# Modulation weights in the ring of weight units of a two-layer trunk kernel

## The chip, the cores and the metric

The kernel runs on one core of a Trainium2 chip. TensorE is PE, and its weight loads are listed apart as PEld; VectorE is DVE, ScalarE is ACT, SyncE is SP, which here does nothing but issue DMAs and wait for their slots. The metric is the device time of one execution in microseconds (us). TensorE's granted clock is given as a share of its full speed: 1.00 is 2.4 GHz, 0.50 is 1.2 GHz, and a value in between is a stretch with both.

## The reference

Two layers act on a prompt tile and a sample tile of 128 rows each, with 2048 channels. All weights are read once, in float32.

```
for l in range(2):
    sh1, sc1, g1, sh2, sc2, g2 = split(silu(cond) @ w_mod[l] + b_mod[l], 6)   # 2048 x 12288, two conditions
    h = rmsnorm(x) * (1 + sc1) + sh1
    q, k, v of A, B, C, and f = split(h @ w_in[l])                            # 2048 x 4352
    outs = attention A (8 heads), B (4 double heads), C (8 heads), Fourier mix of f
    merged = sum_b sigmoid(h @ w_gate[l][b] + b_gate) * (outs[b] @ w_branch[l][b])
    x = x + g1 * (merged @ w_out[l])
    h2 = rmsnorm(x) * (1 + sc2) + sh2
    x = x + g2 * mixture_of_16_experts(h2)                                    # top group, then 2 experts
```

The modulation is a product of two rows (the condition of the prompt and that of the sample) with a matrix of 96 MB for each layer. Its results are wanted late: sh1 and sc1 ahead of the layer's first norm, g1 in the rows of the merge (`gate_rows(32)`), sh2 and sc2 in the second norm, g2 in `gate_rows(80)` after it.

## The kernel before

**Weight units.** A weight matrix comes in units of 512 rows by 512 columns (128 partitions x 4 blocks x 512, 1 MB), four to a chunk of 512 output columns. SP's `load` puts each in one of 4 slots of `raw_w`. ACT rounds it to a high part (L557, two halves), DVE forms the low part (L872, two halves), both into one of 2 split slots, and PE runs 24 matmuls per unit, for each block and tile high x high, low x high and high x low (L1392 to L1394). A slot of `raw_w` comes free once DVE has made the low part (`low_ready`).

**Modulation units.** The matrix of the modulation is 24 chunks of 4 units per layer, 48 chunks and 192 units of 1 MB in all. They are not split: PE multiplies them as they land, four matmuls to a unit (L1412, in `mod_units`), each on its own 32 columns of the array, with the two conditions as weights. A chunk ends with a copy of its sums (`mod_copy`, DVE L879), a turn of four small matmuls on PE (`mod_turn`, L1420) and an add into `mod` (`mod_store`, DVE L885). They have a ring of their own, `mod_w` with 4 slots, in the memory of the split slots; so they are never in flight beside weight units, and `load_mods` waits until the split slots are used up.

**Stages.** Per layer: norm, w_in (8 chunks of 4 units and a last one of half the width), mixers (Fourier, then 12 groups of A, B and C, each a chain of scores, softmax, turn of the weights, values), gates (for each of 4 column chunks and each of 4 branches: 4 units of w_gate and one of w_branch), merge and `gate_rows`, w_out (4 chunks), routing (norm, router, `gate_rows`, sort), experts. Every engine runs its own program in this order. `mod_stage` and `MOD_ORDER` lay down where the chunks go: 8 at the start; in the mixers 14 per layer (2 beside Fourier, 12 beside the groups, one chunk to a group: two units ahead of the turn of the weights, two behind it); in layer 0 also 2 beside the merge, 2 beside its rows and 8 beside norm, rows and sort of the routing; in layer 1 two beside the norm of the routing. `mod_step` on PE and DVE places them there.

Of the kernel before, what the change touches and what calls it, by code (L numbers as in the profile page):

```python
# [37 lines left out]
F32 = mybir.dt.float32  # L38
# [14 lines left out]
MOD_SLOTS = 4  # L53
# [101 lines left out]
def trunk(nc, io, places):  # L155
# [12 lines left out]

    FIRST = 2 * D // COLS

    def mod_stage(l, stage):
        spans = {"fourier": [(l, FIRST, FIRST + 2)], "attention": [(l, FIRST + 2, MODS - 2)]}
        if l + 1 < DEPTH:
            spans |= {"merge": [(l, MODS - 2, MODS)], "mixer rows": [(l + 1, 0, 2)], "norm": [(l + 1, 2, FIRST - 4)],
                      "expert rows": [(l + 1, FIRST - 4, FIRST - 2)], "sort": [(l + 1, FIRST - 2, FIRST)]}
        else:
            spans |= {"norm": [(l, MODS - 2, MODS)]}
        return [(m, c) for m, a, b in spans.get(stage, []) for c in range(a, b)]

    STAGES = ("fourier", "attention", "merge", "mixer rows", "norm", "expert rows", "sort")  # L180
    MOD_ORDER = [(0, c) for c in range(FIRST)] + [m for l in range(DEPTH) for s in STAGES for m in mod_stage(l, s)]
# [9 lines left out]
    with ExitStack() as ctx:  # L191
# [14 lines left out]
        mod_w = place("mod_w", [P, MOD_SLOTS, KB, COLS], at=spot[0] - 4 * MOD_SLOTS * KB * COLS)  # L206
# [35 lines left out]
        mod = place("mod", [P, 2, MODS * 4, 2])  # L242
# [45 lines left out]
        turn_banks, mod_bank = banks[5:7], banks[7]  # L288
# [5 lines left out]
        high_ready, low_ready, unit_used = sem("high_ready"), sem("low_ready"), sem("unit_used")  # L294
        chunk_read, gate_ready = sem("chunk_read"), sem("gate_ready")
        mod_in = [sem(f"mod_in{i}") for i in range(MOD_SLOTS)]
        mod_used, mod_copied, mod_turned, mod_stored = sem("mod_used"), sem("mod_copied"), sem("mod_turned"), sem("mod_stored")
# [81 lines left out]
        def _(sp):  # L379
            at = Cursor()  # L380

            def load(src, width=COLS):
                slot = at.parity("unit", RAW_SLOTS)
                u = at.next("unit")
                need(sp, low_ready, (u - RAW_SLOTS + 1) * HALVES)
                at.next(f"in{slot}")
                sp.dma_start(raw_w[:, slot, :, 0:width], src).then_inc(raw_in[slot], 16)

            def load_mod(l, c):

                for j in range(UPC):
                    slot = at.parity("mod_unit", MOD_SLOTS)
                    need(sp, mod_used, at.next("mod_unit") - MOD_SLOTS + 1)
                    sp.dma_start(mod_w[:, slot, :, :], weight_tile(io["w_mod"], l, bass.ds(c * COLS, COLS), COLS, j)
                                 ).then_inc(mod_in[slot], 16)

            def load_mods(chunks):

                need(sp, unit_used, (at.done("unit") - UPC) * HALVES if chunks else 0)
                for l, c in chunks:  # L400
                    load_mod(l, c)

# [14 lines left out]

            def mod_start(c):
                load_mod(0, c)
            at.rounds(sp, FIRST, mod_start)  # L420
            sp.dma_start(proj[0:36, 0, 0:4 * P], io["pick"][0:36, :]).then_inc(pick_in, 16)
# [6 lines left out]
            for l in range(DEPTH):  # L428
# [29 lines left out]
                def mixers():  # L458
# [8 lines left out]
                    beside = mod_stage(l, "fourier") + mod_stage(l, "attention")  # L467
                    early = 2 + 6
                    load_mods(beside[:early])

# [3 lines left out]
                    load_mods(beside[early:])  # L474


                def gates(n):
                    for b in range(4):
                        for j in range(UPC):
                            load(weight_tile(io["w_gate"], l, bass.ds(n * COLS + b * D, COLS), COLS, j))  # L480
                        if b == 0:
                            r = at.next("bg")
                            if at.first:
                                mixers()
                                sp.wait_ge(bg_clear, l + 1)
# [8 lines left out]
                def merge():  # L494
# [4 lines left out]
                    load_mods(mod_stage(l, "merge") + mod_stage(l, "mixer rows"))  # L499

                def w_out(n):
                    for j in range(UPC):
                        load(weight_tile(io["w_out"], l, bass.ds(n * COLS, COLS), COLS, j))
# [4 lines left out]
                def routing():  # L508
                    sp.dma_start(numbers[:, :], io["numbers"]).then_inc(numbers_in, 16)
                    load_mods(mod_stage(l, "norm") + mod_stage(l, "expert rows") + mod_stage(l, "sort"))  # L510

                def experts(i):
                    for h in range(2):
                        for j in range(UPC):
                            slot = at.parity("unit", RAW_SLOTS)
                            u = at.next("unit")
                            need(sp, low_ready, (u - RAW_SLOTS + 1) * HALVES)
                            for half, name in enumerate(("w_exp_gate", "w_exp_up")):
                                at.next(f"in{slot}")
# [24 lines left out]
        def _(act):  # L544
            at = Cursor()

            def split_high(width=COLS, loads=1):

                slot, part = at.parity("unit", RAW_SLOTS), at.parity("unit", SPLIT_SLOTS)
# [9 lines left out]
            def mods_done():  # L559

                act.wait_ge(mod_used, mods_done.units)
            mods_done.units = UPC * FIRST

# [23 lines left out]

            for l in range(DEPTH):
# [1249 lines left out]
```

## Time and profile before

| | us |
|---|---|
| median of 3 runs | 3095.6 (3092.16 to 3099.6) |
| span of the profiled execution | 3096.7 |
| PE busy | 2766.8 (89% of the span) |
| DVE busy | 1577.1 (51%) |
| ACT busy | 1248.2 (40%) |
| 16 DMA engines busy with the main queue | 66.2% of the span |
| moved | 689.73 MB, mean 223 GB/s |

The profiled execution's span, from the first to the last instruction, is its own time as the trace has it; it lies inside the spread of the three runs, 1.1 us above their median. The shares are means over stages of different kinds, so the rows below are cut by stage. A row of the windows view gives start and end of a stretch, its length, the busy time and instruction count of PE, PEld, DVE, ACT and POOL, then the granted clock, the DMA engines' busy share and the rate. In a timeline, the bracket at a row's end is the time that the engine stood idle ahead of it, and what ended that.

### The profile page before, as it was taken

The numbers are of one execution on the slowest core, as the hardware profiler recorded it, in microseconds if no ns is written. First come the engines' busy times: TensorE is split into PE (matmuls) and PEld (weight loads), VectorE is DVE, ScalarE is ACT, GpSimd is POOL, SyncE is SP. The second block draws the span as 40 slices with busy tenths as digits, with TensorE's granted clock in tenths as the row PEclk, the third lists the DMA queues.
The fourth block names the chain that finished last, engine by engine and source line by source line (L and its number), as shares of the span: only waits on it lengthen the run. The fifth ranks groups of instructions, "written<-read, shape, count | busy, mean of one in ns | idle before, by whom it ended". The sixth has DMA issues, their size and how long they took to land.

```text
span 3096.7 us, 35968 instructions
## 1 busy us (share of the span) xinstructions
PE 2766.8 (89%) x13006; PEld 2069.3 (67%) x13007; DVE 1577.1 (51%) x2058; ACT 1248.2 (40%) x1645; POOL 0.2 (0%) x4
## 2 busy tenths in 40 slices
PE   5799778999998987999978987799999988799997
PEld 1488345888884754787766863478888866677775
DVE  0444333455543545768655433244555454576875
ACT  0244233434442323546544423334444332355654
POOL 0000000000000000000000000000000000000000
PEclk8799889999999978999988999899999988799998
DMA  9755987555558565869764579855555536186974
GB/s 363 246 195 174 339 304 253 182 192 189 187 178 287 177 226 187 269 212 321 257 219 151 193 241 327 298 187 187 190 187 183 187 122 206 46 270 220 323 256 176
DMA packets 428973, 689.73 MB, mean 223 GB/s; under 512 B 26796, under 2 KB 163788, under 8 KB 428208
## 3 DMA queue, kind: packets, MB, share of 16 engines
q1 hardware_dynamic: 428848, 687.96, 66.2%
q8 instruction: 91, 1.49, 0.2%
q14 instruction: 34, 0.28, 0.0%
HBM read 683.45 MB, written 4.46 MB: 222 GB/s over the span
## 4 chain that ended last, share of the span: by engine, by line
PE 75%; DMA 10%; DVE 7%; issue 3%; ACT 3%; DVEq 2%; SPq 1%; ACTq 0%
PE bank L1392 16%; PE bank L1393 15%; PE bank L1394 15%; DMA mod_w<-in_w_mod 10%; PE bank L1412 4%; PE bank L1737 3%; PE bank L1739 3%; PE bank L1738 3%; DVE low_w L872 3%; PE bank L1430 2%; PE bank L1779 2%; PE bank L1780 2%; PE bank L1781 2%; PE bank L1468 1%; ACT high_w L557 1%
## 5 line engine op out<-in xcount | busy, mean ns | idle before, releaser
L872 DVE TENSOR_TENSOR low_w<-raw_w,high_w 128x1024 fp32r<-128x1024 f32 (+1 forms) x912 | 1083.4, 1213 | 795.9 <-ACT high_w L557 790.3
L557 ACT ACTIVATE high_w<-raw_w 128x1024 fp32r<-128x1024 f32 (+1 forms) x912 | 941.8, 1052 | 869.6 <-PE bank L1394 670.9
L1392 PE MATMUL bank<-high_w,in_high 128*128 128x512 f32 (+1 forms) x1856 | 724.6, 390 | 20.4 <-DVE low_w L872 20.4
L1394 PE MATMUL bank<-high_w,in_low 128*128 128x512 f32 (+1 forms) x1856 | 720.6, 388 | 0.0
L1393 PE MATMUL bank<-low_w,in_high 128*128 128x512 f32 (+1 forms) x1856 | 720.6, 388 | 0.0
L1392 PEld LDWEIGHTS bank<-high_w,in_high 128*128 128x128 f32 x1856 | 351.9, 190 | 104.2 <-issue 33.9
L1394 PEld LDWEIGHTS bank<-high_w,in_low 128*128 128x128 f32 x1856 | 351.4, 189 | 71.2
L1393 PEld LDWEIGHTS bank<-low_w,in_high 128*128 128x128 f32 x1856 | 352.0, 190 | 70.0
L1412 PE MATMUL bank<-mod_w,cond 128*32 128x512 f32 x1536 | 257.4, 768 | 94.8 <-DMA mod_w<-in_w_mod 86.2
L1737 PE MATMUL bank<-high_w,in_high 128*128 128x512 f32 x640 | 258.9, 404 | 29.2 <-DVE low_w L872 29.0
L1739 PE MATMUL bank<-high_w,in_low 128*128 128x512 f32 x640 | 251.8, 393 | 0.0
L1738 PE MATMUL bank<-low_w,in_high 128*128 128x512 f32 x640 | 251.8, 393 | 0.0
L1412 PEld LDWEIGHTS bank<-mod_w,cond 128*32 128x32 f32 x1536 | 38.1, 122 | 216.5 <-DMA mod_w<-in_w_mod 134.6
L1737 PEld LDWEIGHTS bank<-high_w,in_high 128*128 128x128 f32 x640 | 121.3, 190 | 69.9 <-DVE low_w L872 41.7
L879 DVE COPY mod_sums<-bank 128x512 f32<-128x512 f32 x48 | 33.2, 691 | 251.9 <-PE bank L1412 251.9
L1739 PEld LDWEIGHTS bank<-high_w,in_low 128*128 128x128 f32 x640 | 121.3, 190 | 26.6
L1738 PEld LDWEIGHTS bank<-low_w,in_high 128*128 128x128 f32 x640 | 121.4, 190 | 23.5
L1779 PE MATMUL bank<-high_w,hid_high 128*128 128x512 f32 x320 | 127.1, 397 | 6.6 <-DVE low_w L872 6.6
L1780 PE MATMUL bank<-low_w,hid_high 128*128 128x512 f32 x320 | 126.3, 395 | 0.0
L1781 PE MATMUL bank<-high_w,hid_low 128*128 128x512 f32 x320 | 126.0, 394 | 0.0
L724 ACT ACTIVATE sig<-bank 128x256 f32<-128x256 f32 (+1 forms) x128 | 55.5, 486 | 172.5 <-PE bank L1394 168.4
L1392 PE MATMUL bank<-high_w,br_high 128*128 128x512 f32 x256 | 99.6, 389 | 0.0
(208 smaller groups left out, 2113.0 us busy)
## 6 DMA issues: line engine op xcount, KB each, us to landing
mod_w<-in_w_mod SPq DMA_DIRECT2D x192, 1024.0 KB, 8.7
raw_w<-in_w_gate SPq DMA_DIRECT2D x128, 1024.0 KB, 5.1
raw_w<-in_w_in SPq DMA_DIRECT2D x64, 1024.0 KB, 5.3
raw_w<-in_w_exp_gate SPq DMA_DIRECT2D x128, 512.0 KB, 4.5
raw_w<-in_w_exp_up SPq DMA_DIRECT2D x128, 512.0 KB, 5.5
raw_w<-in_w_exp_down SPq DMA_DIRECT2D x64, 1024.0 KB, 6.3
raw_w<-in_w_branch SPq DMA_DIRECT2D x32, 1024.0 KB, 5.1
raw_w<-in_w_out SPq DMA_DIRECT2D x32, 1024.0 KB, 5.1
```

What stands on the lines that cost most here:

```text
L557: act.activation(high_w[:, part, ks, 0:width], raw_w[:, slot, ks, 0:width], ACT.Copy).then_inc(high_ready, 1)
L872: dve.tensor_tensor(low_w[:, part, ks, 0:width], raw_w[:, slot, ks, 0:width], high_w[:, part, ks, 0:width].bitcast(F32), ALU.subtract).the ...
L1392: pe.matmul(out, highs[:, kk, t, :], high_w[:, part, k, 0:width], start=start, stop=False)
L1393: pe.matmul(out, highs[:, kk, t, :], low_w[:, part, k, 0:width], start=False, stop=False)
L1394: done = pe.matmul(out, lows[:, kk, t, :], high_w[:, part, k, 0:width], start=False, stop=stop)
L1412: done = pe.matmul(mod_bank[32 * k:32 * k + 32, :], cond[:, j * KB + k, :], mod_w[:, slot, k, :], start=j == 0, stop=j == UPC - 1)
L1737: pe.matmul(out, in_high[:, kk, t, :], high_w[:, part, k, :], start=kk == 0, stop=False)
L1738: pe.matmul(out, in_high[:, kk, t, :], low_w[:, part, k, :], start=False, stop=False)
L1739: done = pe.matmul(out, in_low[:, kk, t, :], high_w[:, part, k, :], start=False, stop=kk == NK - 1)
L1779: pe.matmul(out, hid_high[:, kk, t, :], high_w[:, part, k, :], start=False, stop=False)
L1780: pe.matmul(out, hid_high[:, kk, t, :], low_w[:, part, k, :], start=False, stop=False)
L1781: done = pe.matmul(out, hid_low[:, kk, t, :], high_w[:, part, k, :], start=False, stop=False)
```

## The change

The modulation units lose their own ring and go through the 4 slots of `raw_w`, in line with the weight units, in places written out in three tables. In every chunk of w_in in both layers, and of w_out in layer 0, the order is m0 w0 m1 m2 w1 m3 w2 w3 (m: a unit of modulation, w: of the weight). In the gates it is m0 w0 m1 w1 m2 w2 m3 w3 and then the unit of w_branch, for the first three of the four branches in layer 0 and the first two in layer 1. With the 8 chunks at the start, that makes 8 + 8 + 12 + 4 in or ahead of layer 0 and 8 + 8 in layer 1. Mixers, merge, rows and routing have none. A slot is now freed by a semaphore of its own (`raw_done`): for a weight unit by DVE's low part, for a modulation unit by PE's last matmul on it. `mod_turn` writes to another bank. The matrix is laid out anew ahead of the launch, so that a unit is one block of memory, 8 KB per partition instead of four rows of 2 KB. The load of `pick` stands ahead of the first modulation units, and `mixers` on SP (stores of the new caches, loads of `cache_bc`) stands after the first four units of the gates, not after the first four of w_gate.

```diff
-        mod_w = place("mod_w", [P, MOD_SLOTS, KB, COLS], at=spot[0] - 4 * MOD_SLOTS * KB * COLS)
+    MOD_BEFORE = [(0,), (1, 2), (3,), ()]
+    GATE_MODS = [3] + [2] * (DEPTH - 1)
+    OUT_MODS = [1] + [0] * (DEPTH - 1)
...
             def load(src, width=COLS):
-                slot = at.parity("unit", RAW_SLOTS)
-                u = at.next("unit")
-                need(sp, low_ready, (u - RAW_SLOTS + 1) * HALVES)
-                at.next(f"in{slot}")
+                slot = at.parity("ring", RAW_SLOTS)
+                at.next("ring")
+                need(sp, raw_done[slot], at.next(f"use{slot}") * HALVES)
                 sp.dma_start(raw_w[:, slot, :, 0:width], src).then_inc(raw_in[slot], 16)
...
+            def load_mod(j):
+                m = at.done("mod_chunk")
+                if j == UPC - 1:
+                    at.next("mod_chunk")
+                load(io["w_mod"][bass.ds(m, 1), j].rearrange("a p (k n) -> p (a k) n", k=KB))
...
                         for j in range(UPC):
+                            for m in MOD_BEFORE[j]:
+                                load_mod(m)
                             load(weight_tile(io["w_in"], l, bass.ds((i * 2 + h) * COLS, COLS), COLS, j))
...
                         for j in range(UPC):
+                            if b < GATE_MODS[l]:
+                                load_mod(j)
                             load(weight_tile(io["w_gate"], l, bass.ds(n * COLS + b * D, COLS), COLS, j))
+                            if b == 0 and at.first and j == 1:
+                                mixers()
...
-            def mod_copy():
+            def mod_copy(slot, later):
                 m = at.next("mod_copy")
-                dve.wait_ge(mod_used, m * UPC + UPC)
+                dve.wait_ge(raw_done[slot], (at.done(f"use{slot}") - later) * HALVES)
                 need(dve, mod_turned, m)
                 dve.tensor_copy(mod_sums[:, :], mod_bank[:, :]).then_inc(mod_copied, 1)
...
                 for j in range(blocks // KB):
+                    for m in mods[j] if mods else ():
+                        mod_unit(m)
                     part, u = at.parity("unit", SPLIT_SLOTS), at.next("unit")
+                    slot, use = ring_slot()
+                    at.next(f"in{slot}")
                     for k in range(KB):
                         if k % HALF == 0:
-                            pe.wait_ge(low_ready, u * HALVES + k // HALF + 1)
+                            pe.wait_ge(raw_done[slot], use * HALVES + k // HALF + 1)
...
+                    if j == 2 and mods is MOD_BEFORE:
+                        mod_turn()
...
+            def mod_unit(j):
+                slot, use = ring_slot()
+                if j == 0:
+                    need(pe, mod_copied, at.next("mod_chunk"))
+                pe.wait_ge(raw_in[slot], at.next(f"in{slot}") * 16 + 16)
+                for k in range(KB):
+                    done = pe.matmul(mod_bank[32 * k:32 * k + 32, :], cond[:, j * KB + k, :], raw_w[:, slot, k, :],
+                                     start=j == 0, stop=j == UPC - 1)
+                done.then_inc(raw_done[slot], HALVES)
...
                 for G, (j, b, t, g) in enumerate(GROUPS):
                     if G + 1 < NG:
                         scores(G + 1)
-                    mod_step(2)
                     turn_weights(G)
-                    mod_units(UPC - 2)
                     values(G)
-                    mod_step(0)
...
+    arrays["w_mod"] = np.ascontiguousarray(blocks.transpose(0, 4, 1, 3, 2, 5)).reshape(-1, d // (KB * P), P, KB * COLS)
```

PE's program in the first chunk of w_in, layer 0, after the change, from the chunk's start to the turn (a unit that landed in `raw_w` is multiplied by `cond` for the modulation, and by `in_high` and `in_low` after its split; L1424 is the turn):

```order
L1414 MATMUL bank<-raw_w,cond 32x512 x4
L1391 MATMUL bank<-high_w,in_high 128x512
L1392 MATMUL bank<-low_w,in_high 128x512
L1393 MATMUL bank<-high_w,in_low 128x512
...
L1414 MATMUL bank<-raw_w,cond 32x512 x8
...
L1424 MATMUL bank<-const,mod_sums 128x2 x4
```

m0, the pair m1 and m2, and the turn are new there, with 24 matmuls of a weight unit wherever rows are left out (m3 stands ahead of the third weight unit like m0 ahead of the first); before, PE's rows in w_in are the same triples, with line numbers one higher, without a break. PE's program at the head of the mixers of layer 0, before (L1501, L1508 and L1509 are the Fourier mix, L1430 turns, L1551 the scores, L1590 the values, L1412 and L1420 the modulation):

```order
L1501 MATMUL bank<-const,proj 128x256 x4
L1412 MATMUL bank<-mod_w,cond 32x512 x16
L1508 MATMUL bank<-e_buf,const 128x512
L1509 MATMUL bank<-e_buf,const 128x512
L1501 MATMUL bank<-const,proj 128x256 x4
L1420 MATMUL bank<-const,mod_sums 128x2 x4
L1412 MATMUL bank<-mod_w,cond 32x512 x16
L1508 MATMUL bank<-e_buf,const 128x512
L1509 MATMUL bank<-e_buf,const 128x512
L1420 MATMUL bank<-const,mod_sums 128x2 x4
L1430 MATMUL bank<-const,proj 128x128 x5
```

And after, from the same place to the values of the first group:

```order
L1497 MATMUL bank<-const,proj 128x256 x4
L1503 MATMUL bank<-e_buf,const 128x512
L1504 MATMUL bank<-e_buf,const 128x512
L1497 MATMUL bank<-const,proj 128x256 x4
L1503 MATMUL bank<-e_buf,const 128x512
L1504 MATMUL bank<-e_buf,const 128x512
L1428 MATMUL bank<-const,proj 128x128 x5
L1428 MATMUL bank<-const,cache_a 128x128
L1546 MATMUL bank<-qk_t 128x128 x16
L1428 MATMUL bank<-const,e_buf 128x128 x8
L1585 MATMUL bank<-p_t,cache_a 64x128
```

The modulation is gone from between the steps of the chain. SP's program from the end of w_in to the first gates of layer 0, before:

```order
L387 DMA raw_w<-in_w_gate 128x4x512 [waits low_ready] x4
L466 DMA out_new_attn_k<-proj 128x128 [waits chunk_read]
...
L394 DMA mod_w<-in_w_mod 128x4x512 [waits mod_used,unit_used]
L394 DMA mod_w<-in_w_mod 128x4x512 [waits mod_used] x31
L472 DMA cache_bc<-in_cache_na_k 128x512 [waits pv_done]
L473 DMA cache_bc<-in_cache_na_v 128x512
L394 DMA mod_w<-in_w_mod 128x4x512 [waits mod_used,unit_used]
L394 DMA mod_w<-in_w_mod 128x4x512 [waits mod_used] x23
L488 DMA bg_raw<-in_b_gate 4x512 [waits bg_clear]
```

And after:

```order
L379 DMA raw_w<-in_w_mod 128x2048 [waits raw_done0]
L379 DMA raw_w<-in_w_gate 128x4x512 [waits raw_done1]
L379 DMA raw_w<-in_w_mod 128x2048 [waits raw_done2]
L379 DMA raw_w<-in_w_gate 128x4x512 [waits raw_done3]
L454 DMA out_new_attn_k<-proj 128x128 [waits chunk_read]
...
L456 DMA cache_bc<-in_cache_na_k 128x512 [waits pv_done]
L457 DMA cache_bc<-in_cache_na_v 128x512
L379 DMA raw_w<-in_w_mod 128x2048 [waits raw_done0]
L379 DMA raw_w<-in_w_gate 128x4x512 [waits raw_done1]
L379 DMA raw_w<-in_w_mod 128x2048 [waits raw_done2]
L379 DMA raw_w<-in_w_gate 128x4x512 [waits raw_done3]
```

The 56 modulation loads of the mixers are gone from the queue, and two units of modulation and two of w_gate lie in the ring while the mixers run, where there were four of w_gate.

## Rows read from the trace of the kernel before

**Rows 1.** The page: the chain that ended last, shares of the span by line.
```profile
PE bank L1392 16%; PE bank L1393 15%; PE bank L1394 15%; DMA mod_w<-in_w_mod 10%; PE bank L1412 4%; PE bank L1737 3%; PE bank L1739 3%; PE bank L1738 3%; DVE low_w L872 3%; PE bank L1430 2%; PE bank L1779 2%; PE bank L1780 2%; PE bank L1781 2%; PE bank L1468 1%; ACT high_w L557 1%
```

**Rows 2.** Busy by stretch: PE, PEld, DVE, ACT, POOL; clock, DMA share, GB/s.
```profile
0.00:102.90 102.90, 64.69 (x324) 19.29 (x325) 8.61 (x24) 7.60 (x9) 0.20 (x4) 0.78 1.00 364
102.90:126.40 23.50, 8.38 (x33) 6.04 (x33) 19.86 (x47) 7.41 (x11) 0.00 (x0) 0.52 0.63 184
...
315.20:506.10 190.90, 142.59 (x983) 72.31 (x984) 60.82 (x154) 56.30 (x178) 0.00 (x0) 0.85 0.88 317
506.10:960.30 454.20, 451.47 (x1952) 364.89 (x1952) 228.30 (x207) 182.10 (x195) 0.00 (x0) 1.00 0.58 186
960.30:1012.90 52.60, 38.92 (x208) 13.43 (x208) 16.70 (x51) 12.67 (x20) 0.00 (x0) 0.86 0.86 313
...
1105.70:1225.90 120.20, 91.26 (x527) 51.98 (x527) 53.76 (x164) 31.04 (x49) 0.00 (x0) 0.74 0.60 207
...
1831.20:2026.60 195.40, 145.80 (x984) 73.25 (x984) 60.68 (x154) 56.56 (x178) 0.00 (x0) 0.83 0.86 310
...
2481.90:2506.20 24.30, 16.39 (x48) 8.31 (x48) 13.69 (x43) 11.73 (x19) 0.00 (x0) 0.72 0.00 0
...
2597.90:2696.90 99.00, 72.74 (x366) 50.70 (x367) 51.12 (x157) 30.26 (x48) 0.00 (x0) 0.67 0.23 82
```

**Rows 3.** The chain in the mixers of layer 0, shares by line.
```profile
by line: DMA mod_w<-in_w_mod 54.4%; PE bank L1412 14.4%; PE bank L1551 5.2%; PE bank L1430 2.6%; PE bank L1553 2.4%; PE bank L1420 2.0%; ACT e_buf L676 1.9%; SPq L394 1.8%; PE bank L1587 1.5%; issue 1.5%; SPq L466 1.3%; ACT qk_t L661 1.3%; 
```

**Rows 4.** Timeline, mixers of layer 0: start, duration, instruction, idle before.
```profile
334.42 1.86 PE L1508 MATMUL bank<-e_buf,const 128*128 128x512 f32 x2
...
344.36 1.13 PE L1508 MATMUL bank<-e_buf,const 128*128 128x512 f32 x2
...
355.30 0.16 DVE L1045 TENSOR_TENSOR small<-small 128x4 f32<-128x4 f32 x1 [2.09 <-ACT e_buf L676]
...
363.36 1.05 PE L1420 MATMUL bank<-const,mod_sums 128*128 128x2 f32 x8
...
364.53 0.16 DVE L1045 TENSOR_TENSOR small<-small 128x4 f32<-128x4 f32 x1
```

**Rows 5.** As rows 2: the same 24 score matmuls of branch C, twice.
```profile
441.65:445.88 4.23, 4.23 (x24) 3.26 (x25) 0.00 (x0) 0.00 (x0) 0.00 (x0) 1.00 0.53 196
455.57:463.06 7.49, 7.49 (x25) 5.69 (x24) 2.12 (x4) 1.26 (x1) 0.00 (x0) 0.50 0.54 198
```

**Rows 6.** PE's timeline in the first stage: two modulation units.
```profile
17.76 1.93 PE L1412 MATMUL bank<-mod_w,cond 128*32 128x512 f32 x8 [0.69 <-DMA mod_w<-in_w_mod]
20.47 1.94 PE L1412 MATMUL bank<-mod_w,cond 128*32 128x512 f32 x8 [0.78 <-DMA mod_w<-in_w_mod]
```

**Rows 7.** DMA issues: count, KB each, median us to landing.
```profile
raw_w<-in_w_in SPq DMA_DIRECT2D x64, 1024.0 KB, 5.3
...
x<-in_x_prompt SPq DMA_DIRECT2D x1, 1024.0 KB, 4.9
x<-in_x_sample SPq DMA_DIRECT2D x1, 1024.0 KB, 6.9
```

**Rows 8.** PE's timeline in the sort, layer 0: two periods, with one unit each.
```profile
1202.09 0.72 PE L1684 MATMUL bank<-sort,turned_high 128*128 128x256 f32 x4
...
1205.06 0.72 PE L1684 MATMUL bank<-sort,turned_high 128*128 128x256 f32 x4
```

**Rows 9.** PE's timeline in the sort, layer 1: two periods without units.
```profile
2682.20 0.72 PE L1684 MATMUL bank<-sort,turned_high 128*128 128x256 f32 x4
...
2684.03 0.72 PE L1684 MATMUL bank<-sort,turned_high 128*128 128x256 f32 x4
```

**Rows 10.** PE's timeline: three units back to back.
```profile
339.91 2.78 PE L1412 MATMUL bank<-mod_w,cond 128*32 128x512 f32 x24 [0.26 <-DVE mod L885]
```

**Rows 11.** The page's groups: splitting a weight unit, count, busy, mean ns.
```profile
L872 DVE TENSOR_TENSOR low_w<-raw_w,high_w 128x1024 fp32r<-128x1024 f32 (+1 forms) x912 | 1083.4, 1213 | 795.9 <-ACT high_w L557 790.3
L557 ACT ACTIVATE high_w<-raw_w 128x1024 fp32r<-128x1024 f32 (+1 forms) x912 | 941.8, 1052 | 869.6 <-PE bank L1394 670.9
```

More of the change, by code:

```diff
@@ L241, in trunk @@
         pick = place("pick", [36, 4, P], F32R)
-        mod = place("mod", [P, 2, MODS * 4, 2])
+        mod = place("mod", [P, DEPTH, MODS * 4, 2])
         gains = place("gains", [P, 2 * DEPTH, NK])
@@ L547, in split_high @@
             def split_high(width=COLS, loads=1):
-                slot, part = at.parity("unit", RAW_SLOTS), at.parity("unit", SPLIT_SLOTS)
+                slot, part = at.parity("ring", RAW_SLOTS), at.parity("unit", SPLIT_SLOTS)
+                at.next("ring")
                 u = at.next("unit")
@@ L557, in split_high, with pass_mods @@
                     act.activation(high_w[:, part, ks, 0:width], raw_w[:, slot, ks, 0:width], ACT.Copy).then_inc(high_ready, 1)
-            def mods_done():
-                act.wait_ge(mod_used, mods_done.units)
-            mods_done.units = UPC * FIRST
+            def pass_mods(units):
+                for _ in range(units):
+                    slot = at.parity("ring", RAW_SLOTS)
+                    at.next("ring")
+                    at.next(f"in{slot}")
             def root_mean_square():
@@ L758, in _ @@
                 gate_rows()
-                mods_done.units += UPC * len(mod_stage(l, "merge") + mod_stage(l, "mixer rows"))
-                mods_done()
                 def w_out(n):
                     for j in range(UPC):
+                        if OUT_MODS[l]:
+                            pass_mods(len(MOD_BEFORE[j]))
                         split_high()
@@ L799, in _ @@
                     act.activation(in_high[:, 2 * q:2 * q + 2, :, :].rearrange("p k t n -> p (k t n)"), banks[2][:, :], ACT.Copy).then_inc(sort_stored[0], 1)
-                mods_done.units += UPC * len(mod_stage(l, "norm") + mod_stage(l, "expert rows") + mod_stage(l, "sort"))
-                mods_done()
                 def hid_copy(e):
@@ L865, in split_low @@
             def split_low(width=COLS):
-                slot, part = at.parity("unit", RAW_SLOTS), at.parity("unit", SPLIT_SLOTS)
+                slot, part = at.parity("ring", RAW_SLOTS), at.parity("unit", SPLIT_SLOTS)
+                at.next("ring")
+                at.next(f"use{slot}")
                 u = at.next("unit")
@@ L902, in root_mean_square, with norm @@
                 dve.wait_ge(root_ready, n + 1)
-            def norm(l, which, mod_units=0):
+            def norm(l, which):
                 shift, scale, gain = 48 * which, 48 * which + 16, 2 * l + which
@@ L963, in w_in_pair @@
                 def w_in_pair(i):
-                    for j in range(2 * UPC):
-                        split_low()
-                    at.next("chunk")
-                    at.next("chunk")
+                    for h in range(2):
+                        for j in range(UPC):
+                            pass_mods(len(MOD_BEFORE[j]))
+                            if 3 in MOD_BEFORE[j]:
+                                last = pass_mods.slot
+                            split_low()
+                            if j == 2:
+                                mod_copy(last, 0)
+                        mod_store()
+                        at.next("chunk")
                 at.rounds(dve, IN_CHUNKS // 2, w_in_pair)
@@ L1118, in gates @@
                             at.next(f"merge{l}")
+                        for j in range(2):
+                            pass_mods(mods)
+                            split_low()
+                        if mods:
+                            mod_copy(pass_mods.slot, 0)
                         split_low()
-                        split_low()
-                        split_low()
+                        if mods:
+                            mod_store()
                 at.at[f"merge{l}"] = -1
@@ L1480, in mod_start @@
             def mod_start(c):
-                mod_units(UPC)
+                for j in range(UPC):
+                    mod_unit(j)
                 mod_turn()
```

208 lines of the change are left out of this document (87 added, 121 removed).

## The prediction

> **What bounds the kernel now.** First the page's chain: over 60% of the span are matmuls on weight units, and one tenth is waiting for modulation loads, with 4% more for their matmuls [rows 1]. So there are two kinds of stage, and a mean over the span hides them. The windows, cut at the stages, part them [rows 2]. In the gates of layer 0 PE is busy 451.5 of 454.2 us at clock 1.00 and the DMA engines 0.58 of the time: PE sets the pace, and whatever is put on PE there comes on top. In the mixers (190.9 us in layer 0, 195.4 in layer 1) the DMA engines are busy 0.88 and 0.86 of the time while the clock is below 0.86. The chain inside the mixers of layer 0 says what holds them: 54.4% waiting for modulation loads, 14.4% their matmuls, 2.0% the turns [rows 3]. Mixers, the merge and routing of layer 0 have room on PE and lack bandwidth; w_in, gates and w_out have bandwidth and no room on PE. The change moves 160 of the 192 modulation units (40 chunks) from the former to the latter. The question is which is dearer.
>
> **What the move gives back.** *Mixers.* How long are they bare? I walked the timeline of layer 0 along the chain scores, softmax, turn, values, and left out every stretch in which PE had nothing but modulation to wait for. The first 40.1 us, from 315.2 [rows 2] to the softmax weights of the first group at 355.30, hold two such stretches: the inputs of the two Fourier matmuls at 334.42 and 344.36 had been ready for 15.9 and 4.2 us [rows 4]. That leaves 20.0. The first group, 355.30 to 364.53, takes 9.2, and its modulation work lies under ACT and DVE [rows 4]; the 12 groups so walked are 105.7 in all, from 4.4 to 18.4 each. Sum: 126 us, with PE at 2.4 GHz almost throughout.
>
> It need not stay there. PE would be busy some 41 of these 126 us. The stretches that already run without modulation have this sort of load, and a low clock: 0.52 in the norm of layer 0 (PE busy 8.4 of 23.5), 0.72 in the merge and rows of layer 1 (16.4 of 24.3) [rows 2]. The same 24 score matmuls took 4.23 us at clock 1.00 and 7.49 at 0.50 [rows 5], a factor of 1.77; all of the 41 us at half speed would add 31, and make 157. I take two thirds of that, 147, since the two rows named are on average between the levels, nearer to the lower. Gain 190.9 - 147 = 44 and 195.4 - 147 = 48, together 92 (72 to 134).
>
> What speaks against the change stands in the Trainium skill, "TensorE: Matmul & The Clock Gate", Part 1: the throttled state is the default, and activity releases it. The rows agree (0.52 with PE idle most of the stretch); by that rule alone the mixers would be at 157 each, and the time 20 us longer than my sum.
>
> *Merge and rows of layer 0.* Those of layer 1 are the same work without modulation: 52.6 against 24.3 [rows 2], gain 28.
>
> *Routing.* Layer 0 has 32 units beside it, layer 1 has 8: 120.2 and 99.0 [rows 2]. 24 units with their turns thus cost 21.2, or 0.88 each; by that the bare routing is 92. By the sort, a period with a unit takes 2.97 (1202.09 to 1205.06) [rows 8] and one without 1.83 (2682.20 to 2684.03) [rows 9], so 1.14 each, and 8 of them with two turns at the low clock 0.67 are some 14: bare 85. If the clock stayed up it would be about 79. I take 85: gain 35 + 14 = 49 (35 to 61, by the three values).
>
> *Start.* The 32 units there follow each other at 2.71 us (17.76, 20.47), each ended by its load [rows 6]. Units of 8 KB rows were not in the trace, but x is loaded so: two loads one behind the other landed 4.9 and 6.9 us after their issue [rows 7], and one DMA kind is a little faster than the other. Between nothing and 0.25 us per unit (8 us), I take 6.
>
> Gain in all: 92 + 28 + 49 + 6 = 175 (135 to 231).
>
> **What it costs.** *A unit on PE.* Three back to back take 2.78, so 0.93 each [rows 10]; in the sort, between matmuls of the full array as it will stand now, 1.14 [rows 8, 9]. The new places are of the second kind, so m0 and m3 of a w_in chunk and all four in a gates chunk are 1.14, and the pair m1 m2 is 2.0. *A turn* is 1.05 in its row [rows 4], some of it under its neighbours: 1.0. A w_in or w_out chunk: 1.14 + 2.0 + 1.14 + 1.0 = 5.28; there are 8 + 8 + 4 = 20, so 106. A gates chunk: 4 x 1.14 + 1.0 = 5.56; there are 12 + 8 = 20, so 111. Sum 217; with every unit and turn at 0.93 it is 186.
>
> *The ring.* Where PE needs a weight unit, its load, its high and its low half must be done: 5.3 from issue to landing [rows 7], then 1.05 on ACT and 1.21 on DVE for the first half [rows 11]. In a w_in chunk the slot of w1 was m0's, free only when PE has finished m0. Counted from the chunk's start, PE ends m0 at 1.14; w1 is split at 1.14 + 0.1 + 5.3 + 1.05 + 1.21 = 8.8. PE comes to it after m0, w0, m1 and m2: 1.14 + 5.5 + 2.0 = 8.6. (A weight unit takes about 5.5: the gates' 454.2 over 80 units is 5.68, and holds the bias matmuls too [rows 2].) Likewise w2 in the slot of m1, 15.3 against 15.2. So loads are just late, by some 0.2 twice per chunk: 20 x 0.4 = 8. If loads took as long as the second of x, 6.9, each would be 1.6 later: 20 x 3.6 = 72. The rate that is asked, 8 MB per chunk of some 27 us (310 GB/s), is below what the start moves, 364 [rows 2]. In the gates w_j sits in the slot of w_(j-2), free as soon as DVE has split that, so there is no such wait. I take 8 (0 to 72).
>
> The page "DMA: Bandwidth & Descriptors" of the Trainium skill, Anatomy of one DMA, would give 2.0 us plus the bytes over 436 GB/s, an estimate of 4.4 us per load, where the rows show 5.3 to 6.9. By it the ring would never wait, and the time would be 8 lower.
>
> *Other edits, at nothing.* The copy of the sums and the add to `mod` wait on DVE, ahead of later splits; in w_in the copy stands behind the low part of w2, about the time that PE ends m3, and the low part of w3 has 24 matmuls of w2 to hide under. PE's turn stands behind that same unit, so the copy is done. In the gates the copy is behind w3's low part, and PE has w3 to do before the turn. If a copy came late, PE would wait what remains of it, under 1 us in each of 40 chunks. The first two units of w_gate were in the ring during the mixers before and still are; the other two now load once the mixers are over, while PE works on m0, w0 and m1, w1, more than 13 us against a load of 5.3. The moved load of `pick` and the stores of the caches stand ahead of work that PE reaches tens of us later.
>
> Sum: 217 + 8 - 175 = +50. On the trace's own span of 3096.7 that is 3147; the span lies 1 above the median of the runs shown, so I say **3145**.
>
> **The rivals.** *The clock stays up in the mixers.* Then they take 126 each and the routing 79: gains 65 + 69 + 28 + 61 + 6 = 229 against 225, so 3093, not slower; with units at 0.93 too it is 3062. It decides where the mixers come under 128 us each. For it: the clock was 0.85 with modulation between, and the bare chain is denser than the present one. Against it: 0.52 and 0.72 in the stretches without modulation [rows 2]. *The clock is low throughout.* Mixers 157, routing 92: gains 141, time 3181. For it the norm's 0.52, against it the merge's 0.72. *The ring starves.* Loads of 6.9 us where two ask at once make the 72 above in place of 8, so 3209, or with half of it 3177. For it: the DMA engines would be asked for over 80% of what the start moves. Against it: at the start they deliver 364 GB/s without a gap. *Units on PE are cheap.* If a unit between fp32r matmuls costs 0.93, the sum is 31 lower, 3116; for it rows 10, against it rows 8 and 9, whose place is more alike.
>
> **How the numbers follow.** My forecast with the cheap units as its lower end, 3110 to 3170: 0.55. Clock up: 0.20, of which 0.14 under 3089. Clock low throughout: 0.12. Ring starving: 0.10. What is left, 0.03, is faster for several of the reasons at once. From the case of the clock the range takes in the half from 3070 up, from the low clock and the ring what lies up to 3190: 3070 to 3190. A measurement of this kernel tells a difference from about 0.2%, or 6 us. Faster by more: 0.14 + 0.03 = 0.17. Within it: 0.05, the upper part of the clock case. Slower: 0.78.
>
> **What would show it.** Mixers of 140 to 155 us each, without a wait for a modulation load, and a granted clock of 0.55 to 0.75 there; merge and rows of layer 0 at 24; routing near 85 in both layers. The gates of layer 0 longer by 12 x 5.56 = 67, those of layer 1 by 44, w_in of either layer by 42 to 46, w_out of layer 0 by 21, with clock 1.00. In w_in PE should wait for low parts of w1 and w2 for tenths of a us. A clock near 0.9 in the mixers would turn the sign of the forecast; waits of a us or more at w1 and w2 would say that the ring starves; a period of a modulation unit under 1 us between weight units would say that I overpriced it.

## The result

The changed kernel takes 3201.6 us (median of 4 runs, 3195.9 to 3207.0), the kernel before 3097.6 in the runs beside it: a ratio of 1.0334, 95% interval 1.0307 to 1.0361. It is slower, as forecast, but by 104 us and not by 50, and outside the range, which ended at 3190.

The windows of the changed kernel, cut at the same events as [rows 2]: the start with the first norm, w_in, mixers, gates, merge and routing of layer 0, then mixers, gates and routing of layer 1.

```profile
0.00:120.10 120.10, 70.95 (x356) 23.45 (x357) 27.06 (x67) 13.36 (x18) 0.20 (x4) 0.74 0.83 337
120.10:360.60 240.50, 233.50 (x1184) 168.34 (x1184) 86.54 (x88) 76.67 (x90) 0.00 (x0) 0.99 0.82 294
360.60:498.10 137.50, 78.95 (x423) 60.54 (x423) 47.36 (x123) 53.78 (x175) 0.00 (x0) 0.65 0.04 13
498.10:1053.10 555.00, 526.89 (x2432) 385.79 (x2432) 237.14 (x233) 181.27 (x197) 0.00 (x0) 0.97 0.68 242
1053.10:1074.60 21.50, 16.46 (x50) 8.43 (x50) 12.45 (x41) 8.85 (x15) 0.00 (x0) 0.68 0.00 0
...
1192.10:1275.90 83.80, 58.85 (x287) 49.31 (x287) 49.61 (x152) 30.04 (x49) 0.00 (x0) 0.65 0.00 1
...
1930.40:2068.80 138.40, 81.39 (x425) 62.75 (x425) 47.37 (x124) 53.81 (x175) 0.00 (x0) 0.63 0.04 13
2068.80:2604.20 535.40, 507.27 (x2273) 382.75 (x2273) 234.63 (x225) 182.36 (x197) 0.00 (x0) 0.96 0.64 220
...
2719.60:2803.80 84.20, 59.13 (x287) 50.02 (x287) 49.71 (x152) 30.15 (x49) 0.00 (x0) 0.66 0.00 1
```

Read the lengths first, against [rows 2]. The mixers went from 190.9 to 137.5 and from 195.4 to 138.4, with the DMA engines busy 0.04 and the clock at 0.65 and 0.63. Merge and rows went from 52.6 to 21.5, routing from 120.2 to 83.8 and from 99.0 to 84.2. The gates of layer 0 went from 454.2 to 555.0, 101 more, where the sum had 67; and PE, busy 451.5 of 454.2 before, is now idle for 28 us of them, with a clock of 0.97. Those idle 28 us are no modulation unit's price: they are a wait. The view of PE's waits in that stretch (us in total, times, longest):

```profile
PE bank L1391 <- DVE low_w L858: 25.3, 4, 7.3
PE bank L1414 <- DVE br_low L998: 0.9, 1, 0.9
```

Four times, once per column chunk, PE waits for the low part of w2: 4.4 us in the first chunk, 6.8 to 7.3 in the other three. Layer 1 has the same (25.4 us in 4), and its gates went from 455.3 to 535.4, 80 more, where the sum had 44. The chain through the same stretch names, at 4.5% (25 us), something that the prediction never priced, the load of the gate bias:

```profile
by line: PE bank L1391 27.6%; PE bank L1392 25.4%; PE bank L1393 25.4%; PE bank L1414 8.1%; DMA bg_raw<-in_b_gate 4.5%; PE bank L1609 1.9%; PE bank L1424 1.7%; issue 1.0%; DVE low_w L858 0.9%; SPq L379 0.8%; DVE prod L1082 0.5%; DVEq L1084 
```

The timeline around the second of the four waits, SP's issues first, then the other engines:

```profile
636.22 0.34 SPq L379 DMA_DIRECT2D raw_w<-in_w_mod  x1
...
642.88 0.35 SPq L379 DMA_DIRECT2D raw_w<-in_w_mod  x1
643.41 1.47 SPq L379 DMA_DIRECT2D raw_w<-in_w_gate  x1
644.98 0.72 SPq L473 DMA_DIRECT2D bg_raw<-in_b_gate  x2
```

```profile
648.29 1.07 PE L1414 MATMUL bank<-raw_w,cond 128*32 128x512 f32 x8
...
651.12 0.63 ACT L725 ACTIVATE bg_split<-bg_raw 36x512 fp32r<-36x512 f32 x1 [15.00 <-DMA bg_raw<-in_b_gate]
651.65 3.88 ACT L542 ACTIVATE high_w<-raw_w 128x1024 fp32r<-128x1024 f32 x4
651.78 0.68 DVE L1103 TENSOR_TENSOR bg_split<-bg_raw,bg_split 4x512 fp32r<-4x512 f32 x1 [14.41 <-ACT bg_split L725]
...
656.60 0.80 PE L1391 MATMUL bank<-high_w,in_high 128*128 128x512 f32 x1 [7.25 <-DVE low_w L858]
657.20 0.63 PE L1392 MATMUL bank<-low_w,in_high 128*128 128x512 f32 x1
...
661.89 0.39 PE L1391 MATMUL bank<-high_w,in_high 128*128 128x512 f32 x1
```

SP issues the bias of a column chunk behind the units of its first branch. Before, these were four units of w_gate, each slot free as soon as a unit was split. Now they are eight, and m3 waits for the slot of m1, which PE gives back at 642.7. So the bias goes out at 644.98 and ACT has it at 651.12. ACT takes it ahead of splitting w2, and had stood idle for 15.0 us; DVE too takes it, and a merge, ahead of the low part of w2. PE, done with m2 at 649.35, gets w2 at 656.60. After the wait it starts at the low clock (granted 0.50 from 656.6 to 661.4; 0.63 per matmul, 0.43 apart) and is back at 0.39 per matmul only at 661.9. In the kernel before the same load was out 9.4 us ahead of its use, and ACT came to it without idle time:

```profile
611.93 0.71 SPq L488 DMA_DIRECT2D bg_raw<-in_b_gate  x2
```

```profile
621.38 0.61 ACT L738 ACTIVATE bg_split<-bg_raw 36x512 fp32r<-36x512 f32 x1
```

### The profile page after: what moved, and what is told of

Same layout as the page of the kernel before. It is cut to its first block, busy times and chain, and to the rows that moved or that the text cites. A ratio compares the mean times of both kernels' runs of the same rounds, so it can differ in the third digit from the quotient of the medians.

```text
span 3204.6 us, 35850 instructions
## 1 busy us (share of the span) xinstructions
PE 2809.4 (88%) x13006; PEld 2100.7 (66%) x13007; DVE 1564.6 (49%) x2058; ACT 1233.9 (39%) x1645; POOL 0.2 (0%) x4
## 4 chain that ended last, share of the span: by engine, by line
PE 71%; DVE 9%; DMA 7%; ACT 5%; issue 3%; DVEq 3%; SPq 1%; ACTq 0%
PE bank L1391 14%; PE bank L1392 13%; PE bank L1393 13%; PE bank L1414 4%; DVE low_w L858 3%; PE bank L1732 3%; PE bank L1733 3%; PE bank L1734 3%; PE bank L1428 3%; DMA raw_w<-in_w_in 3%; DMA raw_w<-in_w_mod 2%; PE bank L1776 2%; PE bank L1777 2%; PE bank L1778 2%; ACT high_w L542 2%
## 5 line engine op out<-in xcount | busy, mean ns | idle before, releaser
L858 DVE TENSOR_TENSOR low_w<-raw_w,high_w 128x1024 fp32r<-128x1024 f32 (+1 forms) x912 | 1072.0, 1212 | 765.0 <-ACT high_w L542 758.9
L542 ACT ACTIVATE high_w<-raw_w 128x1024 fp32r<-128x1024 f32 (+1 forms) x912 | 928.5, 1049 | 1047.1 <-PE bank L1393 326.2
L1391 PE MATMUL bank<-high_w,in_high 128*128 128x512 f32 (+1 forms) x1856 | 747.2, 403 | 69.1 <-DVE low_w L858 68.6
L1414 PE MATMUL bank<-raw_w,cond 128*32 128x512 f32 x1536 | 220.9, 662 | 33.1 <-DMA raw_w<-in_w_mod 21.8
L1414 PEld LDWEIGHTS bank<-raw_w,cond 128*32 128x32 f32 x1536 | 34.0, 112 | 128.3 <-issue 70.7
```

Source lines behind the costliest of these rows:

```text
L542: act.activation(high_w[:, part, ks, 0:width], raw_w[:, slot, ks, 0:width], ACT.Copy).then_inc(high_ready, 1)
L858: dve.tensor_tensor(low_w[:, part, ks, 0:width], raw_w[:, slot, ks, 0:width], high_w[:, part, ks, 0:width].bitcast(F32), ALU.subtract).the ...
L1391: pe.matmul(out, highs[:, kk, t, :], high_w[:, part, k, 0:width], start=start, stop=False)
L1414: done = pe.matmul(mod_bank[32 * k:32 * k + 32, :], cond[:, j * KB + k, :], raw_w[:, slot, k, :], start=j == 0, stop=j == UPC - 1)
```

## Experiments

**The bias load early.** Theory A: the bias load is late, and that is the gates' excess. Theory B: w2 itself is late, because modulation units hold the slots. In the changed kernel only the place of one issue is moved:

```diff
-                        if b == 0:
+                            if b == 0 and j == 1:
                                 r = at.next("bg")
...
```

> The changed kernel, with the load of the gate bias (bg_raw) issued after w1 of the first branch of each column chunk, no longer after w3. Theory A, the bias is late: PE's stalls of about 7 us at the third weight unit of every column chunk (8 in all) fall under 1 us, the gates are some 35 us shorter in each layer (520 and 500), and the time is about 3202 - 70 = 3132, 1.1% above the kernel before. Theory B, the weight unit itself is late because modulation units hold its slot: the stalls stay, and the time is 3195 to 3205.

Measured 3135.5, ratio 1.0105 (1.0082 to 1.0128), 2.2% below the changed kernel's. Between the two ratios, and between the two profiled spans (3204.6 and 3133.4), lie 71 us; the medians, taken at different times, are 66 apart. The windows of mixers and gates of layer 0, then of layer 1:

```profile
356.90:494.80 137.90, 81.07 (x426) 62.29 (x426) 47.35 (x124) 53.80 (x175) 0.00 (x0) 0.61 0.04 13
494.80:1017.50 522.70, 519.95 (x2433) 381.05 (x2433) 237.85 (x233) 181.35 (x197) 0.00 (x0) 0.99 0.72 257
1894.10:2034.10 140.00, 83.64 (x423) 63.83 (x423) 47.36 (x123) 53.77 (x175) 0.00 (x0) 0.61 0.04 13
2034.10:2534.40 500.30, 497.50 (x2273) 375.84 (x2273) 235.46 (x225) 182.55 (x197) 0.00 (x0) 0.99 0.69 236
```

And all of PE's waits in the gates of layer 0:

```profile
PE bank L1428 <- DVE merged L1085: 2.8, 1, 2.8
PE bank L1414 <- DVE br_low L998: 0.9, 1, 0.9
```

The gates are 32 and 35 us shorter, 67 together, PE waits for no low part in them any more, and theory A stands, B falls. What is left over the gates before is 522.7 - 454.2 = 68.5 for 12 chunks, 5.7 each, against 5.56 in the sum.

**The bias load late, in the kernel before.** The same cause, without a modulation unit in the ring: the issue goes behind the first unit of the second branch.

```diff
-                        if b == 0:
+                            if b == 1 and j == 0:
                                 r = at.next("bg")
...
```

> The kernel before, with the load of the gate bias issued after the first unit of the second branch, two loads later; no modulation unit is in the ring. Theory A: PE stalls at the third weight unit of each of the 8 column chunks, by 2 to 6 us with what the clock takes to come back, so 16 to 50 us more: 3113 to 3147. Theory B: no change, 3091 to 3104.

Measured 3129.7, ratio 1.0083 (1.0060 to 1.0105). PE's waits in the gates of layer 0, first in the kernel before, then here:

```profile
PE bank L1392 <- DVE low_w L872: 2.0, 1, 2.0
...
PE bank L1393 <- DVE low_w L873: 10.5, 4, 2.9
```

The first of the four is the wait of 2.0 at the start of the gates, which was there before; the other three, 2.8 to 2.9 each, stand at the third weight unit of the second to fourth column chunk. The gates grew by 12 and 9 us, to 466.3 and 464.8. So a late bias alone makes the wait, as theory A has it, though a shorter one than in the changed kernel. Between the two profiled spans (3129.2 and 3096.7) lie 32.5 us; 11 of them are in the mixers of layer 0 (202.0 against 190.9, at a clock of 0.77 against 0.85), whose loads this edit leaves as they were; why is not settled.

**Filler on PE in the mixers.** Is the chain of the mixers slow because PE's clock is low there (theory C), or by ACT and DVE (theory D)? On top of the early bias load:

```diff
...
                         scores(G + 1)
+                    filler(8)
                     turn_weights(G)
+                    filler(8)
                     values(G)
```

> As the kernel with the early bias load, and in every group of the mixers 8 matmuls on data that lie there anyhow ahead of the turn of the weights and 8 ahead of the values, on a bank that nobody reads: no load and no wait is added, only work on PE where it waits. Theory C, the low clock holds the mixers: granted clock there from 0.65 to above 0.85, mixers from 137 to 120 to 128 us per layer, time 20 to 35 below the kernel with the early bias load. Theory D, the chain through ACT and DVE holds them and the clock matters little: mixers 137 to 150, time the same or up to 25 above.

Measured 3116.0, ratio 1.0044 (1.0030 to 1.0057), 19.5 below the kernel with the early bias load. The mixers:

```profile
356.90:488.90 132.00, 108.13 (x619) 83.57 (x619) 47.30 (x124) 53.69 (x175) 0.00 (x0) 0.90 0.04 14
1883.80:2013.70 129.90, 107.55 (x615) 82.54 (x615) 47.26 (x123) 53.66 (x175) 0.00 (x0) 0.89 0.04 14
```

The chain in the mixers of layer 0 (L1495 is the filler):

```profile
by line: PE bank L1495 29.0%; PE bank L1551 11.4%; PE bank L1428 8.3%; PE bank L1590 5.9%; ACT e_buf L665 5.1%; ACT qk_t L650 4.2%; PE bank L1553 4.2%; issue 3.2%; PE bank L1587 2.2%; DVE small L1018 2.1%; ACT L699 1.9%; ACT e_buf L695 1.7%
```

24 to 27 us more work on PE made the mixers 6 and 10 us shorter, with the clock at 0.90 and 0.89 for 0.61; the gates behind them are 2 shorter each (520.3 and 498.1). Theory C holds in kind, and D falls; the mixers end 2 to 4 us above what C gave. The filler itself holds 29.0% of the chain, 38 us, so the 16 us are what the higher clock gave less what the filler took, and the worth of the clock alone is not measured.

**The layout alone.** The kernel before with units of one block, 8 KB per partition:

```diff
-                    sp.dma_start(mod_w[:, slot, :, :], weight_tile(io["w_mod"], l, bass.ds(c * COLS, COLS), COLS, j)
+                    sp.dma_start(mod_w[:, slot, :, :], io["w_mod"][bass.ds(c + l * MODS, 1), j].rearrange("a p (k n) -> p (a k) n", k=KB)
...
```

> The kernel before, with nothing of the change but the layout of the modulation matrix (a unit is one block, 8 KB per partition). Theory E, the modulation loads are the bound at the start and in the mixers and come 0.2 us per unit sooner in 8 KB rows: start 6 shorter, mixers 10 to 14 each, time 3066 to 3075, ratio about 0.991. Theory F, only the start gains, since in the mixers the loads wait for slots as much as for bytes: 3088 to 3093.

Measured 3075.0, ratio 0.9897 (0.9878 to 0.9917). In the profiled execution the start with the norm is 120.7 (before 126.4), the mixers 186.0 and 191.3 (before 190.9 and 195.4). The start gained what was expected, the mixers 4 to 5 and not 10 to 14: by the stages between E and F, by the time at the upper end of E. The ratio is worth 32 us, the stages of this one execution 17; two executions of one kernel differ by as much (3066 to 3082 here), and the difference is not resolved further. This part of the change was worth having by itself.

**Thin modulation matmuls.** With the early bias load, what of the price is PE's own time?

```diff
+                n = 2 if thin else COLS
...
-                    done = pe.matmul(mod_bank[32 * k:32 * k + 32, :], cond[:, j * KB + k, :], raw_w[:, slot, k, :],
+                    done = pe.matmul(mod_bank[32 * k:32 * k + 32, 0:n], cond[:, j * KB + k, :], raw_w[:, slot, k, 0:n],
```

> The kernel with the early bias load, where each matmul of the 160 moved modulation units takes 2 columns in place of 512 (the rest of their product is left out); loads, slots, waits, copies and turns stay. Theory G, what is left of the cost is PE's own time: the gates of layer 0 fall from 523 to about 470, w_in from 238 to 200, and the time by about 160 x 0.85 = 136 to 3000. Theory H, the loads in the shared ring hold PE for a good part of it: w_in stays above 220 and the time above 3050.

Measured 3057.4, ratio 0.9868 (0.9844 to 0.9892). w_in and gates of layer 0, and PE's waits in that w_in:

```profile
120.20:354.20 234.00, 215.42 (x1184) 173.24 (x1184) 86.73 (x88) 77.01 (x90) 0.00 (x0) 0.95 0.83 302
490.80:975.40 484.60, 480.39 (x2433) 380.80 (x2433) 237.75 (x233) 181.27 (x197) 0.00 (x0) 0.99 0.78 278
```

```profile
PE bank L1391 <- DVE low_w L858: 16.6, 9, 2.2
```

Both theories hold, each in its place. In the gates 48 units took 38 us less (0.8 each), as G has it. In w_in the 32 units took only 4.6 less (234.0 against 238.6): PE comes earlier to w1, waits 2 us for it in nearly every chunk, and works through w1 partly at the low clock (0.95 over the stage). So in w_in, with its 8 units to a chunk, the ring (a slot freed, its load, its split) is hardly faster than PE, and the pace of about 28 us per chunk would stand nearly unchanged with cheaper units too. Whether the rate of the loads or the turn-round of one slot sets that pace, this run does not show.

**Another order in w_in.** To tell whether whose slot it is decides that wait:

```diff
-    MOD_BEFORE = [(0,), (1, 2), (3,), ()]
+    MOD_BEFORE = [(0,), (1,), (2, 3), ()]
```

> The kernel with the early bias load, with one table entry moved: w_in and w_out chunks go m0 w0 m1 w1 m2 m3 w2 w3, so that w1 stands in a slot that the split frees early, and only w2 still needs the slot of a modulation unit (m1). Theory I, as the prediction's ring term has it: the wait for w1 (0.84 us in a chunk) goes, the same work stays on PE, w_in 2 to 6 us shorter per layer, in all 5 to 15 below the 3135 of the kernel with the early bias load. Theory J, the ring is bound by the rate of the loads and not by whose slot is free: the wait stands at w2 in place of w1, and the time is the same within 3.

Measured 3133.4, ratio 1.0103 (1.0082 to 1.0125): no difference. PE's waits in w_in of layer 0 are 5.6 us in 9, as they were (5.5 in 9):

```profile
PE bank L1391 <- DVE low_w L858: 5.6, 9, 1.5
```

Now eight of the nine stand at w2; the longest, 1.5, is at w0 of the second chunk, where the changed kernel has one too. Theory I falls. Theory J is not shown by that, for w2 stands in the slot of m1 here, and the prediction's own count has it just late too.

**Sharing out.** If 137 us of mixers hold almost no load (DMA 0.04), and get shorter by work on PE, some modulation belongs there. The shared kernel puts 8 chunks per layer back, through the same ring, with the early bias load; 24 stay between weight units.

```diff
-    GATE_MODS = [3] + [2] * (DEPTH - 1)
+    GATE_MODS = [1] + [0] * (DEPTH - 1)
...
+    MIX_MODS = [[4, 4] + [2] * 12] * DEPTH
...
                         scores(G + 1)
+                    ended = mix_units(2 + G)
                     turn_weights(G)
                     values(G)
+                    if ended:
+                        mod_turn(mod_bank)
```

> The modulation shared out: with the early bias load, 8 chunks per layer go back into the mixers, through the same ring (4 units beside each Fourier half, 2 in each group), and only those 24 that find no place there stay between weight units (8 per w_in, 4 in the gates and 4 in w_out of layer 0). By theories A and C: 32 loads at 2.5 us fit under the mixers' 130, the clock there is above 0.8, so mixers of 125 to 135; gates of layer 0 at 477, of layer 1 as before at 455; the sum is 3103 - 61 - 61 (mixers) - 31 - 51 (merge, routing) - 6 (start) + 24 x 5.9 = 3035. If the loads hold the mixers after all: 150 each, 3070.

Measured 3048.5, ratio 0.9845 (0.9823 to 0.9867). The mixers of layer 0 and the gates:

```profile
358.80:500.80 142.00, 107.82 (x752) 62.96 (x752) 55.80 (x142) 55.37 (x176) 0.00 (x0) 0.86 0.65 242
500.80:974.70 473.90, 471.15 (x2104) 368.85 (x2105) 231.25 (x215) 182.23 (x195) 0.00 (x0) 1.00 0.64 215
```

32 units with their turns make the mixers only 4 longer than with none, while 8 chunks in w_in cost 50. PE waits for no modulation load in them. The length was misjudged by some 7: the clock came back (0.86), but units and turns hold 17.9% of the chain there, 25 us, and took it again.

**More of it in layer 0.** 12 chunks in the mixers of layer 0 and none in its gates: `MIX_MODS` with 40 units over the groups, `GATE_MODS = [0, 0]`.

> As the shared kernel, but 12 chunks in the mixers of layer 0 and none in the gates. 48 loads at 2.5 us are 120 of the mixers' 130: if they flow, mixers of 135 to 140 and the time 15 below the shared kernel; if the groups wait for them as before the change, mixers of 155 to 165 and the time 5 to 10 above it.

Measured 3052.4, ratio 0.9851 (0.9829 to 0.9873), not to be told from the shared kernel. The mixers and gates of layer 0:

```profile
357.00:520.40 163.40, 126.07 (x903) 71.91 (x903) 58.80 (x150) 55.97 (x178) 0.00 (x0) 0.86 0.80 312
520.40:975.70 455.30, 452.57 (x1952) 365.70 (x1952) 228.24 (x207) 182.73 (x195) 0.00 (x0) 0.99 0.58 187
```

Four chunks cost 21 us in the mixers and gave back 19 in the gates. The loads hold the mixers again, as the second case had it: waiting for modulation loads is 20.2% of the chain there.

**From w_in to the gates.** The shared kernel with the 16 chunks of w_in in the gates (`GATE_MODS = [3, 2]`, no modulation unit in w_in).

> The shared-out kernel, with the 16 chunks of w_in put between the units of the gates instead (three of four branches in layer 0, two in layer 1); w_in has none. In the gates a chunk cost 5.6 to 5.7, in w_in 6.2: by that 16 x 0.6 = 9 less, 3039 against 3048.5. If the units in w_in cost what they do on PE alone and the waits came from elsewhere, no difference.

Measured 3040.4, ratio 0.9801 (0.9779 to 0.9823): the best of all, 2% below the kernel before and 5% below the changed one, and 8 us below the shared kernel, where 9 were expected. w_in, mixers and gates of layer 0:

```profile
120.30:309.50 189.20, 188.43 (x865) 157.58 (x865) 82.40 (x72) 78.48 (x88) 0.00 (x0) 0.99 0.59 189
309.50:452.50 143.00, 108.69 (x751) 64.92 (x751) 55.47 (x142) 55.31 (x176) 0.00 (x0) 0.84 0.65 241
452.50:971.90 519.40, 516.18 (x2425) 379.29 (x2425) 236.28 (x231) 180.16 (x195) 0.00 (x0) 1.00 0.73 261
```

w_in is back at 189.2, 49.6 shorter than in the shared kernel, and the gates are 45.5 longer: 6.2 per chunk against 5.7.

## Why the prediction was right and wrong

**The step that failed** is "other edits, at nothing", and with it the gates' price, 67 and 44, which had PE's own time and no wait in it; measured were 101 and 80. The step followed the copy, the turn, `pick` and the cache stores through the queues, but not the bias load, which the diff does not touch. Four modulation units went in ahead of it in SP's queue, and what stands behind them in that queue was not listed. The wait cost 67 us in the gates by the first experiment (71 between the ratios); the second shows such a wait, of 2.8 us in place of 6.8 to 7.3, without the rest of the change. With the bias load early the same change takes 3135.5, inside the 3110 to 3170 that the prediction gave its main case, and 32 above the kernel before (3103.2 in the runs beside it) where the sum had 50. That it comes so near is in part luck: the gains were 24 larger than forecast, and units and waits in w_in and w_out 14 dearer.

**The gains** had the right mechanism and small errors of size. The mixers gave 53.4 + 57.0 = 110, not 92, since bare they take 137.5 and 138.4 and not 147. At a clock of 0.61 to 0.65 they lie near the low level, as forecast (0.55 to 0.75), yet the length did not follow the factor of 1.77 for all of PE's part. The chain in the bare mixers of layer 0:

```profile
by line: ACT e_buf L665 13.2%; PE bank L1546 10.3%; PE bank L1428 9.9%; PE bank L1585 9.3%; ACT p_t L676 5.5%; issue 5.5%; DVE small L1018 5.2%; PE bank L1582 4.8%; DVEq L1019 3.9%; PE bank L1548 3.8%; ACT qk_t L650 2.7%; DVE e_buf L1050 2.
```

PE's five lines in this row make 38.1%, or 52 us, while PE is busy 79: about a third of PE's time, and what the low clock adds to it, lies beside ACT and DVE and lengthens nothing. And the walk was not at full clock: the mixers before had 0.85 [rows 2], and the scores at 0.50 [rows 5], 3.3 us longer, lie in them, so part of the low clock was counted twice. How much each of the two makes of the 10 us is open. Merge and rows gave 31 (28 forecast), routing 36 + 15 = 51 (49), with a bare routing of 84 where 85 was taken. The start with the first norm gave 6 (6).

**The costs on PE.** In the gates, with the bias mended, 5.7 per chunk against 5.56. A unit between two weight units, in the changed kernel:

```profile
505.99 0.39 PE L1393 MATMUL bank<-high_w,in_low 128*128 128x512 f32 x1
506.31 1.06 PE L1414 MATMUL bank<-raw_w,cond 128*32 128x512 f32 x8
507.30 0.50 PE L1391 MATMUL bank<-high_w,in_high 128*128 128x512 f32 x1
507.64 0.39 PE L1392 MATMUL bank<-low_w,in_high 128*128 128x512 f32 x1
```

From the last matmul ahead (505.99) to the second one behind (507.64) are 1.65 us, where two steps of 0.23 would be 0.46: 1.19 for a unit, against 1.14. For w_in and w_out of layer 0 the windows are, before and then (w_out alone) after:

```profile
126.40:315.20 188.80, 188.08 (x864) 157.36 (x864) 82.34 (x71) 78.47 (x88) 0.00 (x0) 0.99 0.58 189
1012.90:1105.70 92.80, 89.91 (x384) 73.91 (x384) 47.63 (x45) 30.91 (x31) 0.00 (x0) 0.97 0.58 187
...
1074.60:1192.10 117.50, 111.20 (x545) 78.79 (x544) 50.98 (x53) 33.33 (x35) 0.00 (x0) 0.99 0.82 289
```

In w_in and w_out the sum had 106 + 8, measured 51.7 + 51.2 + 24.7 = 128 in the changed kernel: PE's waits for low parts there are 6.1, 5.6 and 3.1, or 15 in place of 8, and the units are the rest. The ring term was half the size. Of the ten waits in w_in of layer 0, six stand at w1, three at w2 and one at w0, so the place was right in the main; the reason, that a unit of modulation holds the slot, is not shown, since another order of the slots changed nothing. The loads of w_in landed later than the 5.3 of the sum:

```profile
raw_w<-in_w_in SPq DMA_DIRECT2D x64, 1024.0 KB, 5.7
```

The fit that the prediction quotes from the Trainium skill ("DMA: Bandwidth & Descriptors", Anatomy of one DMA) is given there for DMAs issued by GpSimd, and these are SP's: its 4.4 us and a ring that never waits did not come (5.7 us, and 15 us of waits).

**The rivals.** *The clock stays up* did not happen (0.65). The prediction gave it 42 us in the mixers (147 - 126, twice); the filler brought 16, net of its own time on the chain, and what the clock alone is worth there stays open. *The clock is low throughout*: so it was, nearly, but at a length of 138 and not 157, so the rule of the Trainium skill ("TensorE: Matmul & The Clock Gate", Part 1), that the throttled state is the default, agrees with these rows (0.61 to 0.65), and the price that the prediction drew from the low clock does not. *The ring starves*: not in the gates, where ACT was held by the bias and no wait for a low part is left once the bias comes early; in w_in and w_out it took 15 us, not 72. *Cheap units*: refuted, 1.19 at the place shown and 5.7 per chunk in the gates.

Together: gains of 199 and costs of 309 (gates 101 + 80, w_in and w_out 128) make +110, against 107.9 between the spans (3204.6 and 3096.7); of the missing 58, 70 are the gates' excess, 67 of it the bias load, 14 the units and waits of w_in and w_out, and -24 the larger gains; the 2 that are left lie in stages that the change does not touch.

## What to carry to other kernels

When units are put into a queue, list everything that stands behind them in it up to the next place where another engine waits, also what the diff leaves alone: two loads of 8 KB per column chunk cost more here (67 us) than the units themselves were misjudged by. Here dividing the work between the stages that lack bandwidth and those that lack PE time did better than moving all of it: the mixers carried 8 chunks per layer for 4 us, and each chunk beyond that cost 5 to 6 us wherever it was put. Try the parts of a change alone: the new layout was worth 1% in the kernel before.

## What the hardware showed that was not expected

Work that nobody needs made a stage shorter: 192 matmuls per layer whose results nobody reads raised the granted clock of the mixers from 0.61 to 0.90 and took 6 and 10 us off. A wait of 7 us on PE cost more than itself, since half of the next unit's 24 matmuls ran 0.43 apart in place of 0.23, 2.4 us more. And with 32 units of modulation in the mixers the clock there was 0.86 in place of 0.61, and the stage only 4 us longer, though units and turns kept PE busy for 48 us.
